# First shift and scale of a two-block transformer kernel: computed in column quarters on TensorE's column tiles, with x transposed once and the first projection's chunks ordered by quarters of the depth

## The chip, the cores and the metric

The kernel runs on one core of a Trainium2 chip. The metric is device time in microseconds of that core, median of several runs; lower is better. The engines are TensorE (PE in the rows; its weight loads are PEld), VectorE (DVE), ScalarE (ACT), GpSimd (POOL) and SyncE (SP), which here only issues transfers. All matrix work is float32 data cut in two float32r parts: a product takes three float32r matmuls (high times high, high times low, low times high).

## The reference, cut to what matters

Two transformer blocks on x of shape (1, 256, 2048). Only the start of the first block is touched by the change:

```python
mod = silu(c) @ w_ada + b_ada              # w_ada: 2048 x (6 * 2048), six sections of 2048 columns
shift1, scale1, gate1, shift2, scale2, gate2 = split(mod, 6)
h = rms_norm(x, norm1_w) * (1.0 + scale1) + shift1
proj = h @ w_in                            # 2048 x 7168: q, k, v (1024 each), then four of 1024
# attention over 8 heads | gated linear recurrence over 8 heads, then
x = x + gate1 * (mix @ w_out)
# MLP with shift2, scale2, gate2; then a second block without modulation
```

## The kernel before, in words

**Tiling.** The 256 tokens are two tiles of 128 (T = 2), the depth of 2048 is 16 tiles of 128 (KT = 16). A weight block is 512 output columns. It comes in four chunks of 1 MB, each four depth tiles by 512 columns. A chunk is loaded to `raw`, ACT writes its high part to `w_hi` (`split_hi`, line 255), DVE the rest to `w_lo` (`split_lo`, line 259), and TensorE does 24 matmuls of 512 columns with it (`chunk`, lines 280 to 282): four depth tiles, two token tiles, three products. `raw`, `w_hi` and `w_lo` have four slots each, so SP loads a chunk when the low part four before it is done, and ACT splits it when the chunk four before it has been multiplied. There are 98 blocks: 14 of the input projection (PROJ0), 4 of the output projection (OUT0), then the MLP, the second block's attention and its MLP. TensorE's instructions are written in the order in which they run, and so are those of each other engine; they meet at semaphores.

**The modulation at the start.** Shift and scale of the first norm (2 sections of w_ada, 33.6 MB) are needed before any projection. w_ada's rows are taken as (k p): row 128k + p is on partition p. The columns are done in two halves h. For each half, SP loads 16 pieces of 1 MB (one k; half of the shift and half of the scale columns) into the ring `ada_raw` of four. DVE multiplies most of them by `sc` (silu(c), one value per partition) and adds them up in MS (lines 1137 and 1139, about 2.35 us each). Pieces 3, 7 and 11 of the first half and 7 and 11 of the second go to TensorE (`piece_sums`, line 1733, matmuls with one moving column). MS is then summed over the partitions by TensorE (`step_sums`, line 1743), which gives shift and scale in column form, eight values at a time (`step_modulation`, four steps g; it sets `mod` and `g1`). c comes in through `setup`, which TensorE transposes together with the other small parameters.

**From x to the operand A.** DVE squares and sums x (`first_root`), GpSimd takes the root (line 652), ACT scales x (line 341). TensorE transposes x in eight steps i of two depth tiles (line 330) into PSUM. ACT applies scale and shift out of PSUM (line 368) into `turned` and writes A_hi (line 371); DVE writes A_lo (line 388). Steps 0 to 3 belong to the first half, 4 to 7 to the second; the latter are transposed between the chunks.

**The first group.** `AT0_ORDER` sets the order of the twelve chunks of q, k and v of the first four heads: six with the first half of the depth (HEAD = 6), then six with the second. `at_steps(0)` sets when the squares, norms, transposes and copies of q and k are done. The norm of q is: square on ACT (line 748), sums on DVE (line 1314), root on GpSimd (line 652), scaling on ACT (line 759), rotation on DVE (lines 1307 to 1310), transposes on TensorE (line 1759).

**The rest of w_ada.** gate1, shift2 and scale2 (96 pieces of 0.5 MB) are loaded beside the later projection chunks into the memory of X and added up by DVE (`ada_slot`, lines 1191 and 1194, two pieces a slot; a slot is one chunk). `ada_pieces` says which pieces go to which slot. After 32 pieces and after 96, `parts_rdy` is raised; TensorE waits for the second at position 11 of the output projection. X is then loaded again (line 528), after all 96 pieces have been used, because the output projection adds to it (`out_block`, lines 1443 and 1448, which first waits for x; it frees the PSUM banks in which the block's last chunks are multiplied). SP issues in order: what stands behind a waiting load waits too.

## Time and profile before

| | us |
|---|---|
| median of 3 runs | 2386.78 (2386.42 to 2387.79) |
| the profiled execution | 2390.71 |
| its span, first to last instruction | 2388.7 |
| TensorE busy | 2324.8 (97%) |
| VectorE busy | 1642.0 (69%) |
| ScalarE busy | 1047.8 (44%) |
| moved by the DMA engines | 553.86 MB, 232 GB/s in the mean |

The profile gives a page of totals, and views of the trace: the waits of an engine (who ended them), a table by stretches of time (with the granted TensorE clock as a share of 2.4 GHz, the busy share of the DMA engines and GB/s), the instructions in order of time, the chain of work that ended last, and all instructions of one line. TensorE's matmuls overlap in the rows, so the time of a matmul in a row of them is the distance of starts, not its duration. A float32 matmul or sum shows as two records.

### The profile page before, as it was taken

The page shows a single profiled execution, that of the slowest core. Times are in us where ns is not written, and L with a number is a line of the kernel's source. Part 1 is how long each engine was busy: PE and PEld are TensorE (multiplying, and loading weights), DVE is VectorE, ACT ScalarE, POOL GpSimd, SP SyncE. Part 2 cuts the span into 40 slices and gives each one's busy share as a digit, 9 for nine tenths or more (in the row PEclk, how much of TensorE's full clock was granted, in tenths as well). Part 3 has the DMA queues.
Part 4 walks back from the last instruction along what each step waited for, and adds up shares of the span by engine and source line. Part 5 has one row for each costly group of instructions (what it writes and reads, how often), then busy time and mean ns, then how long its engine had stood idle before and what let it go on. Part 6 is the DMA issues. An engine that isn't in the chain of part 4 may idle for free.

```text
span 2388.7 us, 27685 instructions
## 1 busy us (share of the span) xinstructions
PE 2324.8 (97%) x10698; PEld 1937.2 (81%) x10698; DVE 1642.0 (69%) x1349; ACT 1047.8 (44%) x922; POOL 47.8 (2%) x56
## 2 busy tenths in 40 slices
PE   4899999999999999999999999999999999999999
PEld 3688888888888888888888888878888888888887
DVE  7869999987677676665678456556666565665665
ACT  2245553436444443443344556664443443443442
POOL 0011000001000000000000000000000000000000
PEclk9989999999999999999999999999999999999999
DMA  9989997754877777766665545535566666666663
GB/s 353 372 292 333 351 338 262 264 203 156 284 252 276 261 267 261 242 228 201 214 212 187 178 158 163 170 124 169 201 221 220 211 228 211 214 225 210 212 227 123
DMA packets 258185, 553.86 MB, mean 232 GB/s; under 512 B 12281, under 2 KB 29122, under 8 KB 255426
## 3 DMA queue, kind: packets, MB, share of 16 engines
q1 hardware_dynamic: 257408, 552.72, 67.2%
q8 instruction: 48, 0.79, 0.1%
q10 hardware_dynamic: 706, 0.17, 0.0%
q14 instruction: 23, 0.19, 0.0%
HBM read 533.96 MB, written 18.87 MB: 231 GB/s over the span
## 4 chain that ended last, share of the span: by engine, by line
PE 90%; DVE 4%; DMA 2%; ACT 1%; DVEq 1%; issue 1%; POOL 0%; ACTq 0%; SPq 0%
PE PS L280 27%; PE PS L282 27%; PE PS L281 27%; DMA ada_raw<-in_w_ada_dram 2%; PE PS L1798 1%; DVE w_lo L259 1%; PE PS L1733 1%; PE PS L272 1%; PE PS L274 1%; PE PS L273 1%; PE PS L330 1%; DVE ada_acc L1194 1%; ACT w_hi L255 1%; PE PS L1743 1%; PE PS L1759 0%
## 5 line engine op out<-in xcount | busy, mean ns | idle before, releaser
L259 DVE TENSOR_TENSOR w_lo<-raw,w_hi 128x2048 fp32r<-128x2048 f32 x392 | 897.1, 2290 | 534.8 <-ACT w_hi L255 531.7
L255 ACT ACTIVATE w_hi<-raw 128x2048 fp32r<-128x2048 f32 x392 | 751.4, 1918 | 1047.3 <-PE PS L282 1012.5
L280 PE MATMUL PS<-w_hi,A_hi 128*128 128x512 f32 x2040 | 809.2, 397 | 3.1 <-DVE A_lo L388 1.9
L282 PE MATMUL PS<-w_hi,A_lo 128*128 128x512 f32 x2040 | 798.2, 391 | 0.0
L281 PE MATMUL PS<-w_lo,A_hi 128*128 128x512 f32 x2040 | 797.7, 391 | 0.0
L280 PEld LDWEIGHTS PS<-w_hi,A_hi 128*128 128x128 f32 x2040 | 385.9, 189 | 82.6 <-DVE A_lo L388 2.0
L282 PEld LDWEIGHTS PS<-w_hi,A_lo 128*128 128x128 f32 x2040 | 385.0, 189 | 81.5
L281 PEld LDWEIGHTS PS<-w_lo,A_hi 128*128 128x128 f32 x2040 | 386.0, 189 | 78.4 <-issue 1.0
L280 PE MATMUL PS<-w_hi,H_hi 128*128 128x512 f32 x1024 | 398.6, 389 | 0.4 <-DVE SQ L1639 0.4
L282 PE MATMUL PS<-w_hi,H_lo 128*128 128x512 f32 x1024 | 398.4, 389 | 0.0
L281 PE MATMUL PS<-w_lo,H_hi 128*128 128x512 f32 x1024 | 398.4, 389 | 0.0
L280 PEld LDWEIGHTS PS<-w_hi,H_hi 128*128 128x128 f32 x1024 | 192.2, 188 | 40.9 <-DVE SQ L1639 0.8
L282 PEld LDWEIGHTS PS<-w_hi,H_lo 128*128 128x128 f32 x1024 | 192.2, 188 | 39.9
L281 PEld LDWEIGHTS PS<-w_lo,H_hi 128*128 128x128 f32 x1024 | 192.2, 188 | 39.8
L1194 DVE SCALAR_TENSOR_TENSOR ada_acc<-X,sc,ada_acc 128x1024 f32<-128x1024 f32 x90 | 115.4, 1282 | 8.2 <-issue 2.8
L1563 DVE TENSOR_TENSOR X<-X,PS 128x1024 f32<-128x1024 f32 x60 | 72.6, 1211 | 31.6 <-PE PS L282 31.6
L1563 DVE TENSOR_TENSOR ACC<-ACC,PS 128x1024 f32<-128x1024 f32 x60 | 72.6, 1210 | 28.4 <-PE PS L282 28.4
L652 POOL TENSOR_TENSOR rstd<-ssq,mhalf 128x8 f32<-128x8 f32 (+1 forms) x20 | 41.1, 2056 | 1642.0 <-DVE ssq L443 1377.9
L1139 DVE SCALAR_TENSOR_TENSOR MS<-ada_raw,sc,MS 128x2048 f32<-128x2048 f32 x25 | 58.7, 2350 | 15.7 <-DMA ada_raw<-in_w_ada_dram 15.3
L914 ACT ACTIVATE H_hi<-SQ 128x512 fp32r<-128x512 f32 x64 | 36.9, 625 | 58.1 <-DMA SQ<-H_spill 58.1
L1733 PE MATMUL PS<-sc,ada_raw 128*128 128x1 f32 x160 | 30.0, 322 | 30.6 <-DMA ada_raw<-in_w_ada_dram 30.6
L1733 PEld LDWEIGHTS PS<-sc,ada_raw 128*128 128x128 f32 x160 | 29.9, 291 | 31.2 <-DMA ada_raw<-in_w_ada_dram 17.5
(274 smaller groups left out, 1215.5 us busy)
## 6 DMA issues: line engine op xcount, KB each, us to landing
raw<-in_w_ff_dram SPq DMA_DIRECT2D x128, 1024.0 KB, 5.3
raw<-in_mlp_w_in_dram SPq DMA_DIRECT2D x64, 1024.0 KB, 5.3
raw<-in_mlp_w_out_dram SPq DMA_DIRECT2D x64, 1024.0 KB, 5.1
raw<-in_w_in_dram SPq DMA_DIRECT2D x56, 1024.0 KB, 8.0
X<-in_w_ada_dram SPq DMA_DIRECT2D x96, 512.0 KB, 5.6
raw<-in_sb_w_qkv_dram SPq DMA_DIRECT2D x48, 1024.0 KB, 5.1
ada_raw<-in_w_ada_dram SPq DMA_DIRECT2D x32, 1024.0 KB, 9.9
raw<-in_w_out_dram SPq DMA_DIRECT2D x16, 1024.0 KB, 6.4
```

The costliest lines, as they stand in the source:

```text
L255: act.activation(w_hi[:, j, :, :], raw[:, j, :, :], ACT.Copy).then_inc(hi_rdy, 1)
L259: dve.tensor_tensor(w_lo[:, j, :, :], raw[:, j, :, :], w_hi[:, j, :, :].bitcast(F32), ALU.subtract).then_inc(lo_rdy, 1)
L272: pe.matmul(bank(pair + t), h, w_hi[:, j, k, :], start=first, stop=False)
L280: pe.matmul(bank(pair + t), h, w_hi[:, j, k, :], start=first, stop=False)
L281: pe.matmul(bank(pair + t), h, w_lo[:, j, k, :], start=False, stop=False)
L282: mm = pe.matmul(bank(pair + t), l, w_hi[:, j, k, :], start=False, stop=last)
L652: pool.tensor_tensor(rstd[:, 0:w], ssq[:, 0:w], mhalf[:, 0:w], ALU.pow).then_inc(rstd_rdy, 1)
L914: act.activation(of_token(H_hi, par, t), SQ_turned[:, t], ACT.Copy).then_inc(h_hi, 1)
L1139: ins = dve.scalar_tensor_tensor(out=MS[:, 1 - h, :], in0=sl, scalar=sc[:, k:k + 1], in1=MS[:, 1 - h, :], op0=ALU.mult, op1=ALU.add)
L1194: ins = dve.scalar_tensor_tensor(out=acc, in0=ada_ring[:, q % CH, :], scalar=sc[:, k:k + 1], in1=acc, op0=ALU.mult, op1=ALU.add)
L1563: dve.tensor_tensor(ac, ac, PS[:, b:b + 2, :], ALU.add).then_inc(acc_read, 1)
L1733: mm = pe.matmul(bank(6, at, at + 1), ada_raw[:, k % CH, P * c:P * c + P], sc[:, k:k + 1], start=True, stop=True)
```

## The change

1. **Column quarters.** Shift and scale are computed in four quarters g of 512 columns of each section. w_ada's rows are taken as (p k): row 16p + k is on partition p. SP loads a pair of depth rows k = 2i, 2i + 1 of a quarter as two transfers of 0.5 MB (runs of 2 KB; the distance between partitions is 16 rows of 48 KB) into one slot of `ada_raw`. TensorE sums every pair (`pair_sums`): `sc_rep` is silu(c) repeated 32 times and is the stationary operand, the moving one is 256 columns of w_ada, and the four groups of 256 columns go to four column tiles of the array, 32 columns wide; 8 float32 matmuls a pair, 64 a quarter. DVE takes no part in these sums any more. The sums come out as rows; DVE copies them, TensorE transposes them (`rows_to_columns`), and `step_modulation` picks its values.
2. **c** is loaded by itself in the (p k) order, so silu(c) waits for no transpose. The small parameters and positions are now issued from ACT; SP begins with w_ada.
3. **x transposed once.** TensorE transposes all of x before the first modulation, DVE copies the result back to the memory of X (`copy_turned`), and ACT applies scale and shift from there (`modulate`).
4. **The first group by quarters.** `AT0_ORDER` is now depth quarter by depth quarter, three chunks each, HEAD = 9. Between the chunks of quarter g TensorE does the pair sums of quarter g + 1: three after the first chunk, five after the second, and the transposes in the middle of the third.
5. **What moves with it.** The squares and norms of the first group's q and k come later (steps 10 to 13), q is transposed into bank 6. The first chunk of group 1 waits for `n_mul`. The pieces of gate1, shift2 and scale2 start two slots later and end two slots later: the last four (slots 6 and 7 of the output projection) are added by DVE after the low part of chunk 11, ahead of the output blocks. The ring's first load waits for `a_hi` of step 7.

```diff
-AT0_ORDER = [(b, k) for h in range(2) for b in range(3) for k in (2 * h, 2 * h + 1)]
-HEAD = CH * 3 // 2
+QUARTERS = 4
+AT0_ORDER = [(b, k) for k in range(QUARTERS) for b in range(3)]
+HEAD = 3 * (QUARTERS - 1)
+LOADS_AFTER = {(0, 5): (0,), (0, 7): (1,)}
+for _g in range(1, QUARTERS):
+    LOADS_AFTER.update({(_g, 2): (3 * _g - 1,), (_g, 5): (3 * _g,), (_g, 7): (3 * _g + 1,)})
...
-        return max(0, 2 * (x - HEAD - 1)) - sum(v < x for r in LEVEL_SLOTS for v in r)
+        return max(0, 2 * (x - HEAD)) - sum(v < x for r in LEVEL_SLOTS for v in r)
... (SP)
+            ada = a["w_ada"].rearrange("a (p k) (s n) -> p (a k) s n", p=P, n=D)
+            def load_pair(g, i):
+                n = PAIRS * g + i
+                if n >= CH:
+                    sp.wait_ge(ada_used, n - CH + 1)
+                for k in range(2):
+                    sp.dma_start(ada_raw[:, n % CH, D // 2 * k:D // 2 * (k + 1)].rearrange("p (s n) -> p s n", s=2),
+                                 ada[:, 2 * i + k, 0:2, NC_ * g:NC_ * (g + 1)]).then_inc(ada_in[n % CH], 16)
-            sp.wait_ge(a_tr, KT // 2)
+            sp.wait_ge(a_hi, KT // 2)
-                    if ada and pos < 2 * CH + 2:
+                    if ada and pos < 3 * CH:
... (ACT)
+            def modulate(i):
+                act.wait_ge(g_rdy, i // 2 + 1)
+                act.wait_ge(xT_rdy, i + 1)
+                if i >= 2:
+                    act.wait_ge(a_lo, i - 1)
+                for k in range(2):
+                    c, kt = columns(i, k)
+                    act.activation(turned[:, i % 2, c], xT[:, i, k, :], ACT.Identity, bias=mod[:, SHIFT1, kt], scale=g1[:, kt])
+                act.drain()
+                act.activation(A_hi[:, 2 * i:2 * i + 2, :].rearrange("p k s -> p (k s)"), turned[:, i % 2, :],
+                               ACT.Copy).then_inc(a_hi, 1)
+            split_hi(act, 0, 0)
+            for g in range(QUARTERS):
+                modulate(2 * g)
+                modulate(2 * g + 1)
+                for n in range(3 * g + 1, 3 * g + 4):
+                    split_hi(act, n // CH, n % CH)
... (DVE)
+            first_root()
+            bounds_and_angles()
+            for i in ALL:
+                copy_turned(i)
+            d()
+            split_lo(dve, 0, 0)
+            for g in range(QUARTERS):
+                step_modulation(g)
+                modulate_low(2 * g)
+                modulate_low(2 * g + 1)
+                for n in range(3 * g + 1, 3 * g + 4 if g < QUARTERS - 1 else CH * 3):
+                    split_lo(dve, n // CH, n % CH)
+                if g == 0:
+                    level_masks()
...
+                if isinstance(n, int) and n == 0 and s == steps["norm"][0]:
+                    dve.wait_ge(rstd_rdy, 2)
+                    head_norm(n, 1, KN, 2, 1.0, rotate, not rotate, lambda: dve.wait_ge(n_mul, 1))
+                    turn_heads(n, 0, QN)
+                    return
...
             out_lo(11)
+            ada_slot(CH * OUT0 + 6)
+            ada_slot(CH * OUT0 + 7)
             for b in range(2):
                 split_lo(dve, OUT0 + 3, b)
                 out_block(b)
... (TensorE)
+            def pair_sums(g, i):
+                n = PAIRS * g + i
+                pe.wait_ge(ada_in[n % CH], 32 * (n // CH + 1))
+                for k in (2 * i, 2 * i + 1):
+                    for j in range(4):
+                        c = 4 * QW * (k % 2) + QW * j
+                        mm = pe.matmul(PS[32 * j:32 * j + 32, 6, 0:QW], sc_rep[:, k, :], ada_raw[:, n % CH, c:c + QW],
+                                       start=k == 0, stop=k == KT - 1, tile_position=(0, 32 * j))
+                mm.then_inc(ada_used, 1)
+            for g in range(QUARTERS - 1):
+                at0_chunk(pe, 3 * g)
+                for i in range(3):
+                    pair_sums(g + 1, i)
+                at0_chunk(pe, 3 * g + 1)
+                for i in range(3, PAIRS):
+                    pair_sums(g + 1, i)
+                at0_chunk(pe, 3 * g + 2, between=lambda: rows_to_columns(g + 1))
...
-        return {"square": (8, 10), "norm": (9, 11), "turn": (10, 12), "copy": (11, 12)}
+        return {"square": (10, 11), "norm": (11, 12), "turn": (11, 12), "copy": (13, 13)}
```

## Rows read from the trace of the kernel before

**Rows 1.** Waits of TensorE, whole span: for whom, us in total, times, longest.
```profile
PE PS L1733 <- DMA ada_raw<-in_w_ada_dram: 30.6, 3, 13.4
PE PS L330 <- DVE A_lo L385: 2.0, 1, 2.0
```

**Rows 2.** Table by stretches: stretch, us, granted clock, DMA share, GB/s.
```profile
36.00:38.00 2.00, 1.00 1.03 250
100.00:104.00 4.00, 0.54 1.03 371
124.00:132.00 8.00, 0.93 1.04 405
```

**Rows 3.** TensorE in order of time: start, us, instruction; first and last chunks.
```profile
79.06 0.79 PE L280 MATMUL PS<-w_hi,A_hi 128*128 128x512 f32 x1 [1.91 <-DVE A_lo L388]
...
101.60 0.77 PE L280 MATMUL PS<-w_hi,A_hi 128*128 128x512 f32 x1
...
107.23 0.39 PE L281 MATMUL PS<-w_lo,A_hi 128*128 128x512 f32 x1
...
114.96 0.39 PE L282 MATMUL PS<-w_hi,A_lo 128*128 128x512 f32 x1
...
178.41 1.03 PE L1759 MATMUL PS<-ident,KN 128*128 128x128 f32 x8
```

**Rows 4.** The chain that ended last, from 0 to 40 us: start, us, what.
```profile
3.48 0.43 SPq L490
...
4.98 13.71 DMA ada_raw<-in_w_ada_dram
```

**Rows 5.** All engines in order of time: x on its way to the transposes.
```profile
24.45 2.29 DVE L1072 CUSTOM_DVE_ANT_0 raw<-X 128x2048 f32<-128x2048 f32 x1
...
32.11 5.01 ACT L341 ACTIVATE X<-X,rstd 128x512 f32<-128x512 f32 x8 [17.59 <-POOL rstd L652]
```

**Rows 6.** TensorE in order of time: a float32 matmul of 256 columns, and the next.
```profile
196.88 0.60 PE L1835 MATMUL PS<-kT,qT 128*128 128x256 f32 x2
197.32 0.27 PE L1863 MATMUL PS<-V,AM 128*128 128x129 f32 x1
```

**Rows 7.** All engines in order of time: one step from the sums to A_lo.
```profile
130.24 0.17 DVE L1120 TENSOR_TENSOR mod<-PS,ada_part 128x8 f32<-128x8 f32 x1 [2.51 <-PE PS L1743]
...
132.51 0.69 DVE L388 TENSOR_TENSOR A_lo<-turned,A_hi 128x512 fp32r<-128x512 f32 x1 [1.84 <-ACT A_hi L371]
```

**Rows 8.** Line 472's loads in the last MLP: issue to landing.
```profile
DMA to landing us min/median/max: 4.8/5.2/7.9
```

**Rows 9.** The chain that ended last, 152 to 163 us: the first q's norm.
```profile
153.42 1.22 DVE ssq L1314
...
154.97 3.62 POOL rstd L652
...
158.62 2.19 ACT QN L759 x8
...
162.01 0.28 DVE QN L1310
```

**Rows 10.** DVE in order of time: the output projection before its last chunks.
```profile
503.26 2.67 DVE L1194 SCALAR_TENSOR_TENSOR ada_acc<-X,sc,ada_acc 128x1024 f32<-128x1024 f32 x2
...
526.77 2.29 DVE L259 TENSOR_TENSOR w_lo<-raw,w_hi 128x2048 fp32r<-128x2048 f32 x1
...
532.86 1.23 DVE L1443 TENSOR_TENSOR V<-PS,QN 128x1024 f32<-128x1024 f32 x1 [1.23 <-PE PS L282]
...
537.10 2.29 DVE L259 TENSOR_TENSOR w_lo<-raw,w_hi 128x2048 fp32r<-128x2048 f32 x1
...
555.44 0.69 DVE L1494 TENSOR_TENSOR V<-PS,qT 128x512 f32<-128x512 f32 x1 [1.95 <-PE PS L282]
```

**Rows 11.** TensorE in order of time: chunk 11 of the output projection.
```profile
538.82 0.48 PE L280 MATMUL PS<-w_hi,A_hi 128*128 128x512 f32 x1
```

**Rows 12.** Line 528, the second load of x: issue to landing.
```profile
DMA to landing us min/median/max: 7.6/7.6/7.6
```

More of the change, by code:

```diff
@@ L302, in last_of, with at0_chunk @@
             return max(x for x, (b_, _) in enumerate(order) if b_ == b) + 1
-        def at0_chunk(pe, n):
+        def at0_chunk(pe, n, between=None):
             b, k = AT0_ORDER[n]
-            if b == 0:
-                pe.wait_ge(a_lo, 2 * (k + 1))
             chunk(pe, n // CH, n % CH, pairs[b], lambda i, t: A_hi[:, CH * k + i, P * t:P * t + P],
-                  lambda i, t: A_lo[:, CH * k + i, P * t:P * t + P], k == 0, k == CH - 1)
+                  lambda i, t: A_lo[:, CH * k + i, P * t:P * t + P], k == 0, k == CH - 1, between,
+                  turned=2 * k if b == 0 else None)
         def a_chunk(pe, B, j, pair, turned=None, tokens=range(T)):
@@ L459, in _ @@
         def _(sp):
-            for tile, (r0, n), src in rows[:4]:
-                sp.dma_start(tile[r0:r0 + n, :], src.rearrange("a (r p) -> (a r) p", p=P)).then_inc(params_in, 16)
-            for t in range(T):
-                sp.dma_start(rt[:, 0, t:t + 1].bitcast(I32),
-                             a["positions"][0:1, P * t:P * t + P].rearrange("a (p b) -> (a p) b", b=1)).then_inc(pos_in, 16)
             def load(B, j, src):
                 if isinstance(B, int) and B == 0 and j == 2:
-                    sp.wait_ge(y_rdy, 4)
+                    sp.wait_ge(sum_rdy, 1)
                 if not isinstance(B, int) or B >= 1:
@@ L667, in _ @@
         def _(act):
-            for tile, (r0, n), src in rows[4:]:
+            act.dma_start(c_rows, a["c"].rearrange("a (p k) -> (a p) k", p=P)).then_inc(c_in, 16)
+            for tile, (r0, n), src in rows:
                 act.dma_start(tile[r0:r0 + n, :], src.rearrange("a (r p) -> (a r) p", p=P)).then_inc(params_in, 16)
+                if src is rows[3][2]:
+                    act.wait_ge(c_in, 16)
+                    act.activation(sc[:, :], c_rows, ACT.Sigmoid).then_inc(act_const, 1)
+            for t in range(T):
+                act.dma_start(rt[:, 0, t:t + 1].bitcast(I32),
+                              a["positions"][0:1, P * t:P * t + P].rearrange("a (p b) -> (a p) b", b=1)).then_inc(pos_in, 16)
             act.dma_start(wq_b[:, :], a["q_norm_w"].to_broadcast([P, P])).then_inc(bcast_in, 16)
@@ L841, in _ @@
                 normalise(act, X, X, c)
-            for n in (0, 1):
-                split_hi(act, 0, n)
-            turn_act(act, 0, g1, mod[:, SHIFT1, :], turned, steps=ALL[:4], banks=FIRST)
-            for n in range(2, CH * 2):
-                split_hi(act, n // CH, n % CH)
-            turn_act(act, 0, g1, mod[:, SHIFT1, :], turned, steps=ALL[4:], first=4, banks=SECOND_STEPS,
-                     between={1: lambda: split_hi(act, 2, 0)})
-            split_hi(act, 2, 1)
+            def modulate(i):
[15 more added lines that the diff above has]
+                    split_hi(act, n // CH, n % CH)
             groups = proj_groups()
@@ new lines, in modulate_low @@
+            def modulate_low(i):
+                dve.wait_ge(a_hi, i + 1)
+                dve.tensor_tensor(A_lo[:, 2 * i:2 * i + 2, :].rearrange("p k s -> p (k s)"), turned[:, i % 2, :],
+                                  A_hi[:, 2 * i:2 * i + 2, :].rearrange("p k s -> p (k s)").bitcast(F32), ALU.subtract).then_inc(a_lo, 1)
+            first_root()
+            bounds_and_angles()
+            for i in ALL:
+                copy_turned(i)
+            d()
+            split_lo(dve, 0, 0)
+            for g in range(QUARTERS):
+                step_modulation(g)
[5 more added lines that the diff above has]
+                    level_masks()
@@ L1398, in _ @@
                                 ada_slot(CH * B0 + s - 1)
+                    if i == 1 and s == 0:
+                        at_own(0, PROJ0, CH * 3, True)
                     hg_own(idx, B0, s) if kind == "hg" else at_own(idx, B0, s, True)
@@ L1901, in _ @@
                     else:
-                        if s % CH == 0:
+                        if i == 1 and s == 0:
+                            pe.wait_ge(n_mul, 1)
+                            used[p] = used[p] + 1
+                        elif s % CH == 0:
                             take(p)
```

202 lines of the change are left out of this document (71 added, 131 removed).

## The prediction

> **What bounds the kernel now.** I read the waits of TensorE first. Over the whole span it waits 30.6 us for the pieces of w_ada that it sums itself, and after the start hardly at all: the largest later wait for an operand is 2.0 us [rows 1]. So the kernel is bound by TensorE's own stream of matmuls, except at the start, and what the change is worth is read there. Then TensorE in order of time: the first projection matmul starts at 79.06 [rows 3]. One 512-column matmul takes (114.96 - 107.23) / 34 = 0.227 us at the full clock, so a chunk of 24 takes 5.46. The transposes of the first k stand at 178.41, right behind the first chunk of group 1, so the twelve chunks of group 0 are over, and chunk 12 begins, at 178.41 - 5.46 = 172.95. Twelve chunks need 65.5 us; 172.95 - 79.06 = 93.9 are spent, the rest in sums, transposes and low clock. From 172.95 on both kernels do the same work, so the sum below compares the time at which chunk 12 begins, and then adds what changes later.
>
> **Data first.** Before chunk 12 can end, both kernels need 33.6 MB of w_ada, 2.1 MB of x and 12.6 MB of weights. The table by stretches shows the DMA engines full at 405 GB/s in 124 to 132 us, with loads of the 2 KB runs that the change uses throughout [rows 2]. Before, the first four pieces (4.2 MB) had landed at 4.98 + 13.71 = 18.69, the first one issued at 3.48 [rows 4]; 4.2 MB take 10.4 us at 405 GB/s, so the stream as good as begins 4.8 us after its first issue. With the small loads moved to ACT, SP issues at 0.8, and the stream begins at 5.6. The last pair of the first quarter has 8.4 + 2.1 + 1.0 = 11.5 MB before and in it: 5.6 + 28.4 = 34.0.
>
> **x.** It lands with 4.2 MB, at 16. From the squares to the end of the scaling took 37.12 - 24.45 = 12.7 us [rows 5]: 29, and with the masks that DVE now does first, and the last transposes and copies, 33. So x is just hidden by the data. DVE's share of the sums (30 pieces of 2.35 us) is gone, which costs and gives nothing on the path by itself, because TensorE takes the sums over.
>
> **The pair sum, the disputed price.** No row shows a matmul in a column tile. The nearest is a float32 matmul of 256 columns, 197.32 - 196.88 = 0.44 us in two records [rows 6]. A pair has eight. Bounds: nothing overlaps, 3.5 us; all four tiles overlap fully, 0.9. I take 1.75: the two records of one matmul use the same columns, so if TensorE starts its instructions in order, only the second record of one tile can run beside the first of the next, which halves the time. At the low clock each doubles. The Trainium skill ("TensorE: Matmul & The Clock Gate", Measured speedup vs the span model) gives 2.38 times for three column tiles side by side; by that a pair would cost 1.1 to 1.5 us instead of 1.75. No row here shows it.
>
> **First chunk.** x is over at 33, pairs 5 to 7 follow: 33 + 3 x 1.75 = 38.3. Then the copy of the rows and two transposes, some 1.0, and the path from sums to the first A_lo, 133.20 - 130.24 = 3.0 [rows 7]: 42.3 against 79.06. The clock is low there: at 101.60 to 107.23, with the granted clock at 0.54 in 100 to 104 (half of 2.4 GHz, part of the time) [rows 2, 3], after 4 us of one-column sums, 13 matmuls took 5.63 us, 2.7 more than at the full clock. First chunk over at 42.3 + 5.5 + 2.7 = 50.5.
>
> **A quarter.** Count from the end of its first chunk, t. Three pairs are there: 5.25. A chunk, 5.46. Pair 3 is done at t + 12.5. The ring has four slots, so pair 7 is issued only now, and lands 5.2 us later (a lone load of 1 MB [rows 8]) at 17.7; the 5.2 MB between t and there need 12.9 us and are no tighter. Pairs 4 to 6 are hidden in this. Pair 7, 1.75: 19.5. The last chunk 5.46, with the transposes of the rows in its middle, leaves a gap of 0.5 to the first A_lo of the next quarter; its first chunk 5.46. A quarter is 30.9 us. With pairs of 0.9 us it is 28.8 plus a low-clock start of up to 2.7, so nearly the same. Two quarters: 50.5 + 61.8 = 112.3; then 19.5 + 5.46 + 0.5 and three chunks 16.4: group 0 ends at 154.1.
>
> **Before chunk 12: a new stall.** The first load of group 1 and the ring wait for the last modulation, about 0.9 us into chunk 9 (which begins at 137.7). DVE has slot 9's two pieces ahead of q's sums. Weights, weights, piece, piece land at 5.2 + 2.6 + 1.3 + 1.3 behind that, 11.3 us into the stretch, and the adds end at 12.6. From q's sums to its rotation took 162.29 - 153.42 = 8.9 us [rows 9], GpSimd's root 3.6 of it. So q can be transposed 21.5 us into the stretch, the chunks are over at 16.4: TensorE waits 5.1 us, with chunk 12 behind it. The transposes 0.8, and a low-clock start after the idle time, 2.7: chunk 12 in effect begins at 154.1 + 5.1 + 0.8 + 2.7 = 162.7. Gain so far 172.95 - 162.7 = 10.2. What was queued on SP and is passed (weights, ring) costs nothing more: DVE's lead in w_lo is about two chunks.
>
> **The output projection: given back.** Four adds (two took 2.67 [rows 10]: 5.3) and four passes of about 0.7 over 512 columns (as the one in [rows 7]) move behind the low part of chunk 11, which ends at 529.06. The second load of x waits for the adds, to 534.4, and lands 7.6 later [rows 12], at 542.0; the loads of chunks 13 to 15 stand behind it on SP and land at 544.6, 547.2 and 549.8. DVE: low part of chunk 12 to 539.8, output block 0 from 542.0 (a block is 537.10 - 532.86 = 4.2 [rows 10]) to 546.2, then low, block, low, low: 548.5, 552.7, 555.0, 557.3. TensorE's first token half of chunk 15 can start at 557.3 and end at 560.0; before it ended at 538.82 + 72 x 0.227 = 555.2 [rows 11], and 555.44 is when DVE went on with it [rows 10]. DVE's third block moves its next step to 562.0. So 562.0 - 555.44 = 6.5 us are lost, with no slack shown behind it. Bounds: 0, if only a part of DVE's chain counts, and 8. One collection of sums also moves into the crowded slots of the recurrence: 0.5.
>
> **Sum.** -10.2 + 6.5 + 0.5 = -3.2 us. On the profiled execution 2390.7 - 3.2 = 2387.5; it stands 3.9 above the median, and the difference is the same there: 2386.8 - 3.2 = **2383.6**.
>
> **Rivals.**
> - *The sums cost more than they look (ends slower).* Place: the 24 pairs between the chunks and three before the first. If the column tiles do not overlap (3.5), or they overlap in twos but at the low clock (3.5 again), each further microsecond of a pair costs 24 + 3 = 27: 27 x 1.75 = 47, to 2431. It decides from 1.75 + 3.2 / 27 = 1.87 us a pair. For it: no row shows an overlap, and the one-column sums ran into the low clock. Against: 256 columns stream like a matmul does.
> - *The stalls are smaller (faster).* TensorE's wait before chunk 12, with the low clock behind it (7.8), and the output projection's 6.5 rest on long chains in which each wait is the latest. If two thirds of them are hidden: 2383.6 - 9.6 = 2374.
> - *The new row order slows w_ada (slower).* Partitions now lie 768 KB apart instead of 48 KB. A row shows full DMA engines at only 250 GB/s [rows 2]. At that rate 8.4 MB take 33.6 us instead of 20.7, a quarter 41.4 instead of 30.9: 12.9 + 3 x 10.5 = 44, to 2428. All other full stretches, at 48 KB and 28 KB, show about 400. The Trainium skill ("DMA: Bandwidth & Descriptors", Latency and other measured facts) has the rate fall for row distances of large powers of two, hardly at 512 KiB, to three quarters at 2 MiB; 768 KiB is three times a power of two, so by it the loss is between nothing and a quarter of the rate. No row of this kernel shows such a distance.
>
> **How the numbers follow.** A measurement of this kernel can tell about 0.2%, 4.8 us, from no change: faster is below 2382.0, slower above 2391.6. Chances: the forecast, 2376 to 2390, 0.46 (of this 0.22 below 2382, 0.21 within, 0.03 above); smaller stalls, 2366 to 2377, 0.19; dearer sums 0.25; slower rows 0.10. Faster 0.41, same 0.21, slower 0.38. The range must hold 8 in 10 and takes in most of both sides: 2367 to 2431.
>
> **What would show it.** First projection matmul at 42 (38 to 47); the spacing of the eight matmuls of a pair, 1.75 us; first chunks of quarters about 31 apart; chunk 12 from about 160; a wait of TensorE for DVE of about 5 us before q's transposes; waits for w_lo of chunks 13 to 15 in the output projection. The prediction is wrong if a pair takes over 2 us, if DMA is full at well under 400 GB/s in the first 120 us, or if the waits in the output projection are missing.

## The result, and the profile after

| | before | after |
|---|---|---|
| median, us | 2387.28 (2386.42 to 2388.89, 4 runs) | 2399.64 (2397.06 to 2402.74, 4 runs) |
| the profiled execution | 2390.71 | 2398.92 |
| its span | 2388.7 | 2397.0 |

The ratio is 1.0047, with a 95% interval of 1.0034 to 1.0059: the changed kernel is slower by 0.47%, where 0.13% faster was forecast. The time lies in the range given (2367 to 2431), but on the other side of the kernel before than the forecast, by more than the 0.2% that the prediction calls no change.

The waits of TensorE over the whole span of the changed kernel (for whom, us in total, times, longest), which answer to [rows 1]:

```profile
PE PS L1731 <- DMA ada_raw<-in_w_ada_dram: 35.8, 14, 7.6
PE PS L280 <- DVE w_lo L259: 5.0, 2, 3.4
PE PS L1757 <- DVE QN L1303: 4.7, 1, 4.7
PE PS L272 <- DVE A_lo L1138: 4.4, 4, 3.2
```

TensorE in order of time (start, us, instruction, the idle time ahead of it and who ended it): the last pair of the first quarter, the first matmuls of the four quarters, three stretches of pair sums, and the transposes of the first q and k:

```profile
37.73 1.94 PE L1731 MATMUL PS<-ada_raw,MS 128*32 128x256 f32 x16 [1.57 <-DMA ada_raw<-in_w_ada_dram]
44.05 0.77 PE L272 MATMUL PS<-w_hi,A_hi 128*128 128x512 f32 x1 [3.15 <-DVE A_lo L1138]
79.20 0.47 PE L272 MATMUL PS<-w_hi,A_hi 128*128 128x512 f32 x1 [0.39 <-DVE A_lo L1138]
84.86 2.80 PE L1731 MATMUL PS<-ada_raw,MS 128*32 128x256 f32 x48
100.31 1.07 PE L1731 MATMUL PS<-ada_raw,MS 128*32 128x256 f32 x16 [4.16 <-DMA ada_raw<-in_w_ada_dram]
102.96 1.94 PE L1731 MATMUL PS<-ada_raw,MS 128*32 128x256 f32 x16 [1.58 <-DMA ada_raw<-in_w_ada_dram]
112.84 0.47 PE L272 MATMUL PS<-w_hi,A_hi 128*128 128x512 f32 x1 [0.41 <-DVE A_lo L1138]
144.62 0.47 PE L272 MATMUL PS<-w_hi,A_hi 128*128 128x512 f32 x1 [0.41 <-DVE A_lo L1138]
165.89 1.55 PE L1757 MATMUL PS<-ident,QN 128*128 128x128 f32 x8 [4.69 <-DVE QN L1303]
173.89 1.03 PE L1757 MATMUL PS<-ident,KN 128*128 128x128 f32 x8
```

The first projection matmul is at 44.05, 35.0 us earlier than in [rows 3]. The transposes of k are at 173.89, only 4.5 us earlier. A single pair of traces fixes that gain to a few us at best: in the changed kernel with the adds earlier (below), whose start is the same, the same transposes stand at 178.18, and in the five traces of kernels that start like the one before, at 175.64 to 179.40. A pair of sums (16 records) costs 2.80 / 3 = 0.93 us at the full clock and 1.94 at the lower one.

The output projection. First VectorE (the adds of the last four pieces, then the output blocks), then TensorE's two waits in it:

```profile
523.68 5.45 DVE L1187 SCALAR_TENSOR_TENSOR ada_acc<-X,sc,ada_acc 128x1024 f32<-128x1024 f32 x4
...
536.76 1.23 DVE L1444 TENSOR_TENSOR V<-PS,QN 128x1024 f32<-128x1024 f32 x1 [2.09 <-DMA X<-in_x_dram]
...
547.64 4.49 DVE L259 TENSOR_TENSOR w_lo<-raw,w_hi 128x2048 fp32r<-128x2048 f32 x2
```

```profile
543.54 0.50 PE L280 MATMUL PS<-w_hi,A_hi 128*128 128x512 f32 x1 [1.58 <-DVE w_lo L259]
549.99 0.80 PE L280 MATMUL PS<-w_hi,A_hi 128*128 128x512 f32 x1 [3.39 <-DVE w_lo L259]
...
563.55 1.03 PE L411 MATMUL PS<-ident,ACC 128*128 128x128 f32 x8
```

The transposes at 563.55 (line 411) stood at 560.68 in the kernel before: the lead of 4.5 us, 5.3 by the low part of chunk 11 (521.47 for 526.77), has become a lag of 2.9, so 8.2 us were lost in this stage. Not all of it is waiting: behind the wait of 3.39 us the clock is low, and the 48 matmuls up to the transposes take 13.56 us instead of 48 x 0.227 = 10.9.

That leaves the rest. The forecast let both kernels do the same work from there on, and by their instructions they do. Yet the lag grows evenly in both MLPs, by 0.21 us with every pair of blocks: from 3.0 us at 633 to 6.0 at 1256, down by 1.0 in the second block's attention, and on to 8.3 at the end. TensorE does not wait there. Its matmuls themselves are slower, but only in every second block. Below are the first and the last of a block's 96 matmuls: in the changed kernel one of the second product (operands H) and the one of the first product behind it (operands A), then one of the second product in the kernel before:

```profile
705.42 0.39 PE L280 MATMUL PS<-w_hi,H_hi 128*128 128x512 f32 x1
...
727.16 0.39 PE L282 MATMUL PS<-w_hi,H_lo 128*128 128x512 f32 x1
727.39 0.39 PE L280 MATMUL PS<-w_hi,A_hi 128*128 128x512 f32 x1
...
748.92 0.39 PE L282 MATMUL PS<-w_hi,A_lo 128*128 128x512 f32 x1
```

```profile
702.08 0.39 PE L280 MATMUL PS<-w_hi,H_hi 128*128 128x512 f32 x1
...
723.61 0.39 PE L282 MATMUL PS<-w_hi,H_lo 128*128 128x512 f32 x1
```

With A it takes 21.53 us in both kernels, with H 21.74 to 21.75 in the changed one and 21.53 before. In the trace's finer times a triple of matmuls takes 680 ns, and with H in the changed kernel 687.

What differs is an address. c left the tile `colB`, so the change cut it from 73 to 57 columns of four bytes. SBUF tensors are laid out one behind the other; everything behind `colB` moved down by 64 bytes. `A_hi`, `A_lo`, `raw`, `w_hi` and `w_lo` lie ahead of it and did not move. `H_hi` and `H_lo`, the stationary operands of the second product, began at byte 171008 = 334 x 512 and at 350 x 512, which a padding tile (`to_line_b`) saw to (by the sizes of the tiles, `H_hi` lies 299 x 512 bytes behind `A_hi`, which has its own padding tile); now they begin 64 bytes below such multiples.

So there are three theories to test: the start gains less because the ring of four slots, and not the rate, sets the quarter; the output projection loses 8 us by the late adds; the MLPs lose 6 to 7 us by the address. For the last, the rival is that loops or instructions lie elsewhere. The edits below move the other tensors behind the padding as well (`ACC`, `RE`, `SQ` and the attention's); that it is `H_hi` and `H_lo` is read from the blocks, since only those that read H become slower.

### The profile page after: what moved, and what is told of

It reads as the page before. It is cut to its first block, busy times and chain, and to the rows that moved or that the text cites. A ratio compares the mean times of both kernels' runs of the same rounds, so it can differ in the third digit from the quotient of the medians.

```text
span 2397.0 us, 28260 instructions
## 1 busy us (share of the span) xinstructions
PE 2332.8 (97%) x10994; PEld 1911.2 (80%) x10994; DVE 1588.8 (66%) x1331; ACT 1047.7 (44%) x922; POOL 43.7 (2%) x56
## 4 chain that ended last, share of the span: by engine, by line
PE 90%; DVE 3%; DMA 3%; ACT 1%; DVEq 1%; issue 1%; ACTq 0%; SPq 0%; POOL 0%
PE PS L280 27%; PE PS L281 27%; PE PS L282 27%; DMA ada_raw<-in_w_ada_dram 2%; PE PS L1796 1%; PE PS L272 1%; PE PS L1731 1%; PE PS L274 1%; DVE w_lo L259 1%; PE PS L273 1%; PE PS L1757 1%; ACT w_hi L255 1%; PE PS L329 0%; DMA X<-in_w_ada_dram 0%; PE PS L1861 0%
## 5 line engine op out<-in xcount | busy, mean ns | idle before, releaser
L280 PE MATMUL PS<-w_hi,A_hi 128*128 128x512 f32 x2008 | 796.9, 397 | 6.3 <-DVE w_lo L259 5.0
L282 PE MATMUL PS<-w_hi,A_lo 128*128 128x512 f32 x2008 | 784.9, 391 | 0.0
L281 PE MATMUL PS<-w_lo,A_hi 128*128 128x512 f32 x2008 | 784.6, 391 | 0.0
L280 PEld LDWEIGHTS PS<-w_hi,A_hi 128*128 128x128 f32 x2008 | 379.3, 189 | 88.7 <-DVE w_lo L259 5.8
L282 PEld LDWEIGHTS PS<-w_hi,A_lo 128*128 128x128 f32 x2008 | 378.6, 189 | 80.5
L281 PEld LDWEIGHTS PS<-w_lo,A_hi 128*128 128x128 f32 x2008 | 379.3, 189 | 76.7 <-issue 1.0
L281 PE MATMUL PS<-w_lo,H_hi 128*128 128x512 f32 x1024 | 403.4, 394 | 0.0
L1566 DVE TENSOR_TENSOR ACC<-ACC,PS 128x1024 f32<-128x1024 f32 x60 | 72.6, 1211 | 30.7 <-PE PS L282 30.4
L1731 PE MATMUL PS<-ada_raw,MS 128*32 128x256 f32 x512 | 41.3, 467 | 35.8 <-DMA ada_raw<-in_w_ada_dram 35.8
L1731 PEld LDWEIGHTS PS<-ada_raw,MS 128*32 128x32 f32 x512 | 16.4, 125 | 56.5 <-DMA ada_raw<-in_w_ada_dram 38.0
L272 PE MATMUL PS<-w_hi,A_hi 128*128 128x512 f32 x104 | 42.0, 404 | 5.9 <-DVE A_lo L1138 4.4
```

What stands on the lines that cost most here:

```text
L272: pe.matmul(bank(pair + t), h, w_hi[:, j, k, :], start=first, stop=False)
L280: pe.matmul(bank(pair + t), h, w_hi[:, j, k, :], start=first, stop=False)
L281: pe.matmul(bank(pair + t), h, w_lo[:, j, k, :], start=False, stop=False)
L282: mm = pe.matmul(bank(pair + t), l, w_hi[:, j, k, :], start=False, stop=last)
L1566: dve.tensor_tensor(ac, ac, PS[:, b:b + 2, :], ALU.add).then_inc(acc_read, 1)
L1731: mm = pe.matmul(PS[32 * j:32 * j + 32, 6, 0:QW], sc_rep[:, k, :], ada_raw[:, n % CH, c:c + QW], start=k == 0, stop=k == KT - 1, tile_posi ...
```

## Experiments

Each was timed beside the kernel before on the same chip, and the ratio is to that. The changed kernel's ratio of 1.0047 is the mark; 0.01% is 0.24 us. Differences in us are taken from the ratios, because the kernel before had medians of 2389.4 to 2390.0 beside these runs and 2387.3 beside the changed kernel.

**The address in the changed kernel.**

```diff
-        colA, colB = sb("colA", [P, P]), sb("colB", [P, NRB])
+        colA, colB = sb("colA", [P, P]), sb("colB", [P, 73])
```

> The changed kernel, with colB allocated at its old width of 73 columns (only 57 are used). Nothing else differs, so that every tensor behind colB in SBUF, H_hi and H_lo among them, lies where it lay in the kernel before. Theory A (addresses): the 64 bytes by which the change moved H_hi and H_lo make the matmuls of the MLP's second products slower (a triple of matmuls 687 ns instead of 680); the loop's period of two blocks falls from 43.74 back to 43.52 us, and the kernel takes 2399.6 - 6.2 = 2393.4 us. Theory B (the loops' instructions lie elsewhere in the stream, or the stream is slower for another reason): no difference, 2399.6 us and 43.74 us.

Measured: 2391.95 us, ratio 1.0011 (1.0002 to 1.0020). All matmul blocks are back at 21.53:

```profile
700.95 0.39 PE L280 MATMUL PS<-w_hi,H_hi 128*128 128x512 f32 x1
...
722.49 0.39 PE L282 MATMUL PS<-w_hi,H_lo 128*128 128x512 f32 x1
```

It gives 0.36%, 8.6 us, more than the 6.2 expected; the intervals leave room for 6. The two traces, 9.0 us apart, show where the rest is: 6.4 in the MLPs, 1.5 ahead of the transposes of k (see the last section), and 2.5 in the output projection, where in this trace the clock falls ahead of the second wait, which is then shorter (2.20 us for 3.39), and is up again behind it; 1.5 go the other way in the second block's attention. Only the MLPs' part is shown to be the address.

**The address alone, in the kernel before.**

```diff
-        to_line_b = sb("to_line_b", [P, 50])
+        to_line_b = sb("to_line_b", [P, 34])
```

> The kernel before, with the padding to_line_b cut from 50 to 34 columns, so that H_hi, H_lo and all tensors of that region lie 64 bytes lower, as in the changed kernel. No instruction differs but in addresses. Theory A (addresses): the MLP loops slow down to 43.74 us for two blocks, 2387.3 + 6.2 = 2393.5 us. Theory B: no difference, 2387.3 us and 43.52 us.

Measured: 2396.28 us, ratio 1.0031 (1.0019 to 1.0043), 7.4 us slower, with no instruction changed. An H block takes 21.75, an A block (not shown) 21.53:

```profile
700.96 0.39 PE L280 MATMUL PS<-w_hi,H_hi 128*128 128x512 f32 x1
...
722.71 0.39 PE L282 MATMUL PS<-w_hi,H_lo 128*128 128x512 f32 x1
```

The two MLPs have 32 H blocks: 32 x 0.22 = 7.0 us, 6.4 where the lag is read before and behind both MLPs, since a few blocks have waits in them. Theory A holds, and theory B falls.

**Other shifts.** The same padding at 18 and at 42 columns: 128 and 32 bytes lower.

> The kernel before with the padding to_line_b cut from 50 to 18 columns: H_hi, H_lo and the tensors of that region lie 128 bytes lower. If what counts is where a row of a stationary tile begins within 128 bytes, the second products of the MLP run at 680 ns a triple as before, and the time is that of the kernel before; if it counts within 256 or 512 bytes, 687 ns a triple or more, and 6 us above it.

> The kernel before with the padding to_line_b cut from 50 to 42 columns: H_hi, H_lo and the tensors of that region lie 32 bytes lower. If every start off the line costs the same, 687 ns a triple, as with 64 bytes; if 64-byte pieces count, more than 687 ns.

Measured, one execution each beside 2389.96 of the kernel before: 2406.36 (128 bytes) and 2411.61 (32 bytes). The H blocks with 128 and then with 32 bytes, 22.08 and 22.17 us:

```profile
700.83 0.40 PE L280 MATMUL PS<-w_hi,H_hi 128*128 128x512 f32 x1
...
722.91 0.40 PE L282 MATMUL PS<-w_hi,H_lo 128*128 128x512 f32 x1
```

```profile
704.65 0.39 PE L280 MATMUL PS<-w_hi,H_hi 128*128 128x512 f32 x1
...
726.82 0.39 PE L282 MATMUL PS<-w_hi,H_lo 128*128 128x512 f32 x1
```

32 x 0.55 = 17.6 and 32 x 0.64 = 20.5 us: the blocks account for the 16.4 and 21.6 that were measured. So the first reading of the 128-byte run, by which 128 bytes would be free, is out; so is the first of the 32-byte run, that every start off the line costs the same. The A blocks, which did not move, took 21.57 us with 128 bytes and 21.53 with 32. Of the starts tried only a multiple of 512 bytes, the length of a row of the 128-column stationary tile, runs at full speed (128 and 32 bytes were timed once each, but the block times come from all of a trace), and the cost does not fall in order with the distance. Which rule is behind it stays open; 256 bytes was not tried.

**The late adds alone, in the kernel before.**

```diff
-        return max(0, 2 * (x - HEAD - 1)) - sum(v < x for r in LEVEL_SLOTS for v in r)
+        return max(0, 2 * (x - HEAD - 3)) - sum(v < x for r in LEVEL_SLOTS for v in r)
...
-                    if ada and pos < 2 * CH + 2:
+                    if ada and pos < 3 * CH:
...
             out_lo(11)
+            ada_slot(CH * OUT0 + 6)
+            ada_slot(CH * OUT0 + 7)
```

> The kernel before, with this one part of the change alone: the pieces of gate1, shift2 and scale2 start and end two slots later, the last four behind the low part of chunk 11 of the output projection. Theory (this part costs 8 us in the output projection, whatever the start looks like): 2387.3 + 8 = 2395.3 us, with TensorE waiting for w_lo of the last chunks. Rival (the loss needs the other parts): 2387.3 us, within 2.

Measured: 2396.29 us, ratio 1.0028 (1.0017 to 1.0040), 6.7 us slower. TensorE's waits are those of the changed kernel, and its transposes of line 412 move from 560.68 to 567.50; here too the clock is low behind the second wait (the 48 matmuls take 12.60 us):

```profile
548.45 0.50 PE L280 MATMUL PS<-w_hi,A_hi 128*128 128x512 f32 x1 [1.51 <-DVE w_lo L259]
554.90 0.80 PE L280 MATMUL PS<-w_hi,A_hi 128*128 128x512 f32 x1 [3.43 <-DVE w_lo L259]
```

**The adds earlier, in the changed kernel.**

```diff
+            ada_adds(CH * OUT0 + 6)
             out_lo(9)
             ada_collects(CH * OUT0 + 5)
+            ada_adds(CH * OUT0 + 7)
             out_lo(10)
             hg_stage(1, OUT0 - 4, 11)
+            ada_collects(CH * OUT0 + 7)
             turn_dve(dve, 1, gmix, **mix_part(3))
             out_lo(11)
-            ada_slot(CH * OUT0 + 6)
-            ada_slot(CH * OUT0 + 7)
```

> The changed kernel, with the adds of the last four pieces of w_ada moved in VectorE's order: slot 6's ahead of the low part of chunk 9, slot 7's ahead of that of chunk 10, their collection behind the recurrence's last stage, instead of all of them behind the low part of chunk 11. Theory (the output projection's loss is that late adds hold up the reload of x and VectorE's blocks): TensorE's waits of 1.6 and 3.4 us for w_lo before the last chunks go, and the kernel takes 2399.6 - 8 = 2391.6 us. Rival (the loss is from the low clock or from the recurrence's own chain, which the adds now would lengthen): within 1 us of 2399.6, or slower.

Measured: 2391.92 us, ratio 1.0009 (1.0000 to 1.0018), 0.38% or 9 us less. VectorE had been idle for 4.9 us between the low parts of chunks 9 and 10 (504.6 to 509.5). The four adds now take that room, and the first output block waits for TensorE again, no longer for x:

```profile
506.67 2.67 DVE L1187 SCALAR_TENSOR_TENSOR ada_acc<-X,sc,ada_acc 128x1024 f32<-128x1024 f32 x2
...
511.46 2.67 DVE L1187 SCALAR_TENSOR_TENSOR ada_acc<-X,sc,ada_acc 128x1024 f32<-128x1024 f32 x2
...
531.93 1.23 DVE L1444 TENSOR_TENSOR V<-PS,QN 128x1024 f32<-128x1024 f32 x1 [1.27 <-PE PS L282]
```

The waits for `w_lo` are gone, and so is the rival. What goes with them is the low clock behind them, where a run has it.

**Address and adds together.** The changed kernel with the edits of the first and the last experiment so far, to see whether the two are all of the loss.

> The changed kernel with colB at 73 columns and the last adds of w_ada's pieces earlier, and nothing else: what the change brings at the start stays. If the two causes are all that makes the changed kernel slower, and they add up, it runs as far ahead of the kernel before as its start is: about 5 us faster than before, ratio 0.998. If they overlap, or a third loss is hidden behind them: no faster than before, ratio 1.000 or above.

Measured: 2383.01 us, ratio 0.9977 (0.9968 to 0.9986). The two add up within their intervals (0.36% and 0.38% off 1.0047 would give 0.9973), and what is left of the change, 0.23% or 5.5 us, is its gain at the start, with the ring at its old address; the trace has the transposes of k at 172.85, 5.6 us earlier than before.

**Why the start gains only that: the ring.** One edit spreads the pair sums, another adds a fifth slot in the memory of `ada_acc`:

```diff
-                at0_chunk(pe, 3 * g)
-                for i in range(3):
+                at0_chunk(pe, 3 * g, between=lambda: pair_sums(g + 1, 0))
+                for i in (1, 2, 3):
                     pair_sums(g + 1, i)
-                at0_chunk(pe, 3 * g + 1)
-                for i in range(3, PAIRS):
+                at0_chunk(pe, 3 * g + 1, between=lambda: pair_sums(g + 1, 4))
+                for i in (5, 6, 7):
```

```diff
-                if n >= CH:
-                    sp.wait_ge(ada_used, n - CH + 1)
+                if n >= CH + 1:
+                    sp.wait_ge(ada_used, n - CH)
```

> The changed kernel, with the eight pair sums of a quarter spread over its first two chunks: one in the middle of each of them, three behind each, instead of three behind the first and five behind the second. Theory (the quarter is set by the ring of four slots, which stands full while TensorE multiplies): slots come free earlier, TensorE's waits for w_ada fall by about 10 us in all, three quarters take about 30 instead of 33.5 us, and the kernel takes 2399.6 - 10 = 2389.6 us. Rival (the rate of the transfers sets the quarter): within 2 us of 2399.6.

> The changed kernel, with a fifth slot of the ring for w_ada's pairs, in the memory of ada_acc, which is unused until slot 9. Theory (the ring of four sets the quarter): 1 MB more is under way or waiting, TensorE's waits for w_ada fall by 6 to 10 us, and the kernel takes about 2399.6 - 8 = 2391.6 us. Rival (the rate sets the quarter): within 2 us of 2399.6.

Measured: spread, 2392.40 us, ratio 1.0015 (1.0005 to 1.0024), 7.6 us less than the changed kernel; five slots, 2390.19 us, 1.0004 (0.9995 to 1.0013), 10 us less. TensorE's waits for w_ada fall from 35.8 to 29.3 and 30.4 us, and the three quarters take 30.3 and 30.1 us in the mean instead of 33.5. In five traces that keep the ring and the order of the sums (the changed kernel, the two kernels with the old address, the adds and the norm earlier) that mean is 33.5 to 34.7, so the fall is more than their scatter, and the ring was the limit. The waits fell by less than expected (6.5 us for 10 by spreading, 5.4 for 6 to 10 by the fifth slot). Both together:

> The changed kernel with both edits of the quarter, the fifth slot and the spread pair sums. Either alone took 0.32 and 0.43% off the changed kernel. If both shorten the same waits until the transfers are full (405 GB/s): together 0.55 to 0.6%, ratio to the kernel before 0.999 (1.0047 - 0.0055 to 0.006). If they add up: 0.75%, ratio 0.997.

Measured: 2386.53 us, ratio 0.9991 (0.9982 to 1.0000), 0.56% less: they shorten the same waits, as expected, and do not add up.

**The rival: the distance of the rows.**

```diff
-            ada = a["w_ada"].rearrange("a (p k) (s n) -> p (a k) s n", p=P, n=D)
+            ada = a["w_ada"].rearrange("a (k p) (s n) -> p (a k) s n", p=P, n=D)
```

> The changed kernel, with the rows of w_ada for shift1 and scale1 taken as (k p) again, 48 KB apart instead of 768 KB, while c keeps its (p k) order: the sums pair values of c with other rows of w_ada, all else is as in the changed kernel. Theory (the distance of the rows costs nothing, the ring sets the quarter): within 2 us of 2399.6, first chunks of quarters still 33.5 us apart. Rival of the prediction (the distance slows the transfers): the quarters shorten to about 30 us, and the time falls by about 10 us.

Measured: 2401.12 us, ratio 1.0044 (1.0027 to 1.0061): no gain (the kernel's shift and scale are wrong numbers, its work is the same). The first chunks of the quarters stand 35.2 us apart in the mean, not 33.5 as expected and not 30. Below, the table by stretches (stretch, us, busy us and instructions of each engine, granted clock, DMA share, GB/s), first of the changed kernel, then of this one:

```profile
40.00:60.00 20.00, 16.64 (x110) 11.98 (x114) 6.45 (x7) 7.05 (x8) 0.00 (x0) 0.83 0.85 305
60.00:80.00 20.00, 14.04 (x106) 8.35 (x99) 6.83 (x17) 5.23 (x8) 0.00 (x0) 0.83 1.05 399
80.00:100.00 20.00, 16.15 (x142) 10.98 (x140) 5.78 (x4) 5.65 (x4) 0.00 (x0) 1.00 0.84 311
```

```profile
60.00:80.00 20.00, 13.83 (x98) 8.09 (x88) 6.82 (x17) 4.63 (x6) 0.00 (x0) 0.74 1.05 394
80.00:100.00 20.00, 16.73 (x144) 11.60 (x144) 5.28 (x3) 5.37 (x4) 0.00 (x0) 0.98 0.83 305
```

With rows 768 KB apart full engines move 399 GB/s, with rows 48 KB apart 394, and in both kernels the engines stand partly idle in other stretches. So the rival falls. The Trainium skill ("DMA: Bandwidth & Descriptors", Latency and other measured facts) lists lower rates for row distances that are large powers of two. 768 KB is three times such a power, and no loss is seen at it here; the distances that the page lists were not run.

**The price of the pair sums.**

```diff
-                for k in (2 * i, 2 * i + 1):
-                    for j in range(4):
+                for j in range(4):
+                    for k in (2 * i, 2 * i + 1):
```

> The changed kernel, with the eight matmuls of a pair in the order of column tiles (0, 0, 1, 1, 2, 2, 3, 3) instead of (0, 1, 2, 3, 0, 1, 2, 3); the sums are the same. If TensorE starts its matmuls in order and a tile takes one at a time, a pair takes 5 steps of 0.44 us, 2.2 us, instead of 0.93. By the prediction's price, 27 us for each further microsecond of a pair, the kernel then takes 2399.6 + 27 x 1.27 = 2434 us. Theory now (five of eight pairs of a quarter stand ahead of the transfer that ends it, the others are beside waits for w_ada): about 15 x 1.27 = 19 us, 2419 us. If the order costs nothing, 2399.6 us.

Measured: 2398.39 us, ratio 1.0037 (1.0022 to 1.0051), against an expected 2419 or 2434. Three pairs take 2.85 us; the changed kernel has rows of 2.80 and 2.85:

```profile
86.36 2.85 PE L1731 MATMUL PS<-ada_raw,MS 128*32 128x256 f32 x48
```

The order costs nothing, so in this kernel a matmul that stands behind another of its own tile does not hold up the other tiles. In the changed kernel's trace four records start 7 ns apart, and each four 216 ns after the four before; here they start 13 to 31 ns apart, and each four again 216 ns after the last. What a dearer sum would have cost is not shown, since no run made it dearer.

**The norm of the first q.**

Besides this line, ScalarE's two waits ahead of the squares now count one chunk more than the step, since q and k end with chunks 9 and 10.

```diff
-        return {"square": (10, 11), "norm": (11, 12), "turn": (11, 12), "copy": (13, 13)}
+        return {"square": (9, 10), "norm": (10, 11), "turn": (11, 12), "copy": (13, 13)}
```

> The changed kernel, with the squares of the first group's q and k one step earlier on ScalarE and VectorE (steps 9 and 10, each one waiting for its own last chunk) and their norms at steps 10 and 11. Theory (TensorE's wait of 4.7 us before q's transposes comes from the place of q's sums in VectorE's and ScalarE's order, behind a low part and two pieces of w_ada): the wait falls to about 1.2 us, and the kernel takes 2399.6 - 3.5 = 2396.1 us. Rival (the chain from square to rotation is set by transfers or by GpSimd's root, or another wait takes its place): within 1 us of 2399.6.

Measured: 2398.49 us, ratio 1.0038 (1.0023 to 1.0054), 2 us less than the changed kernel by the ratio and 1.1 by the medians, which lies between theory and rival and within the noise. TensorE's wait for q fell from 4.69 to 1.05 us as forecast. Part of that came back a stage later as waits for the softmax of single heads, 3.0 us where the changed kernel has 0.4:

```profile
162.90 1.09 PE L1757 MATMUL PS<-ident,QN 128*128 128x128 f32 x8 [1.05 <-DVE QN L1303]
```

```profile
PE PS L1848 <- ACT E L829: 3.0, 2, 2.0
```

**All five edits.**

> The changed kernel with five edits together: colB at 73 columns, the last adds of w_ada's pieces earlier, the norms of the first group earlier, the pair sums spread, and the fifth slot. If the five causes are apart from each other: 2399.6 - 7.7 - 7.7 - 3.5 - 12 = 2368.7 us. If spreading and ring shorten only the same waits, or if what they gain is lost again before chunk 12: 2376 to 2381 us.

Measured: 2370.34 us (2369.28 to 2370.87), ratio 0.9919 (0.9906 to 0.9933): 0.8% faster than the kernel before. By the ratios, 0.9977 of the two edits, less 0.56% of ring and spreading and 0.09% of the norm, gives 0.9912. The time is near the first forecast (2368.7), although the ring and the spreading do shorten the same waits: the 12 us put down for the two were already less than their sum. It is the change with five repairs, not the change itself. The transfers are now full from 40 to 120, so that the rate is the limit there:

```profile
40.00:60.00 20.00, 18.31 (x132) 12.08 (x136) 5.97 (x4) 6.49 (x8) 0.00 (x0) 0.91 1.05 407
60.00:80.00 20.00, 16.85 (x112) 11.15 (x109) 10.30 (x20) 8.54 (x9) 0.00 (x0) 0.91 1.05 406
80.00:100.00 20.00, 19.22 (x166) 12.41 (x164) 5.25 (x6) 4.06 (x6) 0.00 (x0) 1.00 1.05 403
100.00:120.00 20.00, 18.79 (x161) 11.82 (x160) 7.39 (x5) 6.83 (x6) 0.00 (x0) 1.00 1.05 407
```

## Why the prediction was wrong, point by point

- **First chunk at 42.3:** 44.05. 1.8 us late, within 38 to 47; the transposes of x ended at 32.4 for a forecast of 33.
- **A pair, 1.75 us:** 0.93 (1.94 at the lower clock). The lower of the two bounds was right; the reason for halving (order of start) was wrong. The total hardly felt it, since the last pair of a quarter waits for its transfer. The rival of dear sums is out: it needed 1.87 us a pair at least.
- **A quarter, 30.9 us:** 35.2, 33.6 and 31.8 between first chunks. The forecast's own steps with a pair of 0.93 us give 26.7 (it says 28.8; the 11.5 MB of a quarter need 28.4 at 405 GB/s). What was too small is the landing of the last pair, put down as a lone load of 5.2 us. In the second quarter its two loads were issued at 94.43 and 94.84, right behind pair 3 as the forecast has it, but the later one landed only at 102.92, 8.1 us after its issue, because the loads ahead of it were still under way. The engines had stood nearly idle while the ring was full, and were full from 88 us on (stretch, as above):

```profile
84.00:88.00 4.00, 4.00 (x55) 2.25 (x54) 2.44 (x2) 0.68 (x1) 0.00 (x0) 1.00 0.23 76
88.00:92.00 4.00, 4.00 (x19) 3.28 (x18) 0.00 (x0) 0.00 (x0) 0.00 (x0) 1.00 1.00 345
96.00:100.00 4.00, 0.15 (x4) 0.00 (x0) 0.49 (x1) 1.91 (x1) 0.00 (x0) 1.00 1.06 405
```

  TensorE waits 4.16 us ahead of pair 6 and 1.58 ahead of pair 7, and behind that the clock is low (0.50 from 104 to 108), which costs about 3 us more in this quarter. In all, the fourth quarter's first chunk starts 100.6 us behind the first one's, where the forecast has 95.4 (three quarters, and 2.7 for the low clock of the first chunk): 5.2 us too few, the first of the mis-sized terms.
- **Wait before q's transposes, 5.1 us:** 4.69. Right.
- **Low clock behind it, 2.7 us:** 1.3 in the chunk and 0.4 in the transposes ahead of it.
- **Gain before chunk 12, 10.2 us:** 4.5 by the transposes of k in this pair of traces, 5.7 less than forecast: the quarters, and the late first chunk.
- **Output projection, 6.5 us lost:** 8.2. VectorE's steps came as forecast, less the lead of 5.3: four adds, x late, block 0 at 536.76, two waits for `w_lo` before the last chunks. The 0.5 us for one more collection did not show. What the forecast did not have is the low clock behind the second wait, 2.5 us against the traces without it; and that is not a fixed price. Eight traces have this wait, of 3.39 to 3.44 us each. In five of them (the changed kernel, late adds alone, rows 48 KB apart, the other order of tiles, ring and spreading together) the clock was low behind it and the 48 matmuls took 12.60 to 13.82 us; in three (norm earlier, spreading alone, fifth slot alone) it stayed up and they took 11.02 to 11.06. The two matmuls behind the wait in the kernel with the norm earlier, 0.34 us from start to start where the changed kernel has 0.59:

```profile
548.33 0.50 PE L280 MATMUL PS<-w_hi,A_hi 128*128 128x512 f32 x1 [3.44 <-DVE w_lo L259]
548.67 0.40 PE L281 MATMUL PS<-w_lo,A_hi 128*128 128x512 f32 x1
```

  From the transposes of k to those of line 411 or 412 the kernel before took 382.3 us, the changed one 389.7, the two with the ring or spreading edit and no low clock 387.3. So the lateness itself costs 5 us net, and that the total came near 6.5 + 0.5 (7.4) is partly luck. The rival that two thirds of the stalls are hidden is out.
- **"From 172.95 on both kernels do the same work":** this is the step that failed. It is right for the instructions and wrong for their duration: it put the MLPs at nothing, and the start address of the stationary operands costs 6.4 us there in the profiled executions (7.4 in the kernel before with the shift alone). With the old address the changed kernel comes out at 1.0011 (first experiment), within the 0.2% that the prediction calls no change. No row of before could price it; the diff shows `NRB` getting smaller, and the padding tiles stand in the code. The other half of the miss is the start, 5.7 us too good; either of the two alone would have turned the forecast's 3.2 us of gain into a loss. The prediction gave 0.38 to slower, but by dear sums or slow rows, and neither happened: that it gave slower a fair chance is luck.

In the profiled executions: -4.5 (start) - 0.8 (to the low part of chunk 11) + 8.2 (output projection) + 3.0 (first MLP) - 1.0 (second attention) + 3.4 (second MLP) = +8.3, as measured. The 1.0 us in the attention is the clock again. Ahead of the last transposes before the second block's output projection TensorE waits 2.03 us in both kernels; in the kernel before the clock is low behind it, and seven matmuls take 3.12 us where in the changed kernel they take 1.72. First the kernel before, then the changed one:

```profile
1584.70 0.75 PE L330 MATMUL PS<-ident,MIX 128*128 128x128 f32 x4 [2.03 <-DVE A_lo L385]
```

```profile
1591.04 0.66 PE L329 MATMUL PS<-ident,MIX 128*128 128x128 f32 x4 [2.03 <-DVE A_lo L384]
```

The medians are 12.4 apart, as the profiled run of the kernel before lay 3.4 above its median and that of the changed kernel 0.7 below.

## What to carry to other kernels

When a diff resizes any on-chip tensor, look at what is allocated behind it: two tiles of equal instructions can differ in speed by their start address, and a uniform drift without waits, in only some of the blocks, is how it shows. Small work that is moved "two slots later" must be followed to its last slot, where it meets a stage with no slack; an idle gap of that engine a few instructions earlier may take it for nothing. A wait for a transfer is cured by more slots or earlier release only until the transfers are full. Two single traces can differ by some us in stages that the edit does not touch, through the clock behind a short wait: look there before giving such a difference to the edit.

## What the runs showed of the hardware

- **Start address of a stationary operand.** H blocks of 96 matmuls took 21.53 us at a multiple of 512 bytes, 21.75 at 64 bytes below one, 22.08 at 128 and 22.17 at 32. The Trainium skill ("SBUF — State Buffer", Specifications (TRN2)) gives cachelines of 16 bytes; all four starts are multiples of 16, so by that rule no difference would be expected; the trace does not agree, and the measurement decides.
- **Column tiles.** Eight float32 matmuls of 256 columns into four column tiles took 0.93 us, where one on the full array takes 0.44 [rows 6]: four run side by side almost without loss, one record of each every 216 ns, in either order of the tiles. The Trainium skill ("TensorE: Matmul & The Clock Gate", Measured speedup vs the span model) has 2.38 times for three tiles; here, worked out from the rows, four give 8 x 0.44 / 0.93 = 3.8. No run here has three tiles.
- **Transfers into a shifted ring.** `ada_raw` moved by the 64 bytes too. From 60 to 80 us, with full engines, the three kernels with the old address moved 406 GB/s, the seven others with the (p k) rows 397 to 400. In the kernel before, whose transfers there are of 1 MB, the two traces with the old address have 417 and 418, the three shifted ones 414 to 416. No run isolates it. It may be the 1.5 us that the first experiment's trace gains at the start, but traces of equal starts differ by more.
- **The clock behind a short wait.** The same wait of 3.4 us in a stream of 512-column matmuls left the clock low for the next 7 to 14 matmuls in five traces (granted 0.50 from 550 to 554 in the changed kernel, which is 1.2 GHz) and up in three (1.00 from 549 to 553 with the norm earlier), and a wait of 2.03 us left it low in one kernel and not in the other. The price where it happened was 1.0 to 2.8 us.
